# A two-block model: one distance table, ten kept half tiles of weights, and a ring of seven gathers

## Chip, cores and metric

One core of one Trainium2 chip. The metric is the device time of one launch in microseconds, as the median of several runs. One launch computes everything below.

## The reference, cut to what matters

Two blocks of two layers on 256 tokens of width 1024, in float32. The first block (sparse attention, a second attention, two MLPs) is not touched by the change. The second block alternates a mixer and a layer of experts:

```python
for i in range(2):                                  # DEPTH
    shift, scale, gate = ada_mod(c, ada_w[i, 0], ada_b[i, 0])
    h = x * scale + shift
    f = short_conv_mixer(h, ...) if i == 0 else diff_attention(h, ...)
    x = layer_norm(ALPHA * x + gate * f, ...)
    shift, scale, gate = ada_mod(c, ada_w[i, 1], ada_b[i, 1])
    f = peer_ffn(x * scale + shift, ...)
    x = layer_norm(ALPHA * x + gate * f, ...)

# diff_attention, per head h and part p (8 heads, two softmaxes each)
s = einsum('qd,kd->qk', q, k) - slopes[h] * (qpos - kpos)    # slopes[h] = 2**-(h+1)
p = softmax(where(qpos >= kpos, s, -inf)); a = p[0] - lam * p[1]
o = rms_norm(a @ v) ...; return o @ w_o

# peer_ffn: 8 heads choose 16 of 16384 experts each, for every token
act = gelu(einsum('td,thkd->thk', x, u[idx]))
return einsum('thk,thkd->td', g * act, v[idx])
```

Each token thus reads 128 rows of u and of v in either layer; u and v stand side by side in one table of 8 KB rows.

## The kernel before

Every engine has its own program, written out by hand in `build`; semaphores order them. Tokens lie in two tiles of 128.

**Dense part.** Until about 814 us into the span TensorE works through 59 tiles of weights (512 columns each), which SP loads chunk by chunk into `wring` (two tiles deep, loop at L542 to L550). GpSimd meanwhile loads 96 pieces of `ada_w` into a ring of three buffers (L585); the third lies in the memory of `alibi`, and `ada_used` counts the pieces that VectorE has used (L2076). ScalarE loads the distance tables `alibi` once that count is 96 (L1932, L1933). There are eight tables of 128 x 256, one for each head; VectorE adds one to the scores in `masked` (L2639).

**Slots.** The experts' work is 512 slots, in the order layer 0 tile 0, layer 0 tile 1, layer 1 tile 0, layer 1 tile 1, each of 128. For slot s GpSimd gathers one expert's row for each of the 128 tokens, 1024 KB, into buffer s % RING of `g_ring` (`gather`, L596 to L607); VectorE forms the dot products (L2722); ScalarE applies the gelu and the gate and spreads the coefficient on a diagonal (L1740 to L1745); TensorE multiplies the diagonal by the row's other half into a sum in PSUM (`slot`, L1127) and frees the buffer (`slot_used`). GpSimd gathers slot s + RING only then. RING is 8. The first gathers wait for two more things: slot 6 for `hrow_done`, slot 7 for `ln_done`, because the buffer of slot 7 lies where the layer norm before it still works (L610 to L614).

**Parts beside the slots.** The second mixer and the second experts' query projection are cut into 58 parts for each token tile, and `parts_due` gives the slot at which each part has its turn: tile 0 beside slots 128 to 255, tile 1 beside slots 256 to 383. TensorE runs parts three slots ahead (PE_AHEAD). Among the parts are 24 half tiles of weights, 1024 KB each (`half_tile`, L1157 to L1168): 0 to 11 for q, k and v, then attention, then 12 to 15 for the output projection, then 16 to 23 for the queries of the experts. In this trace halves 0 to 11 of tile 0 run at 1190 to 1266 us and of tile 1 at 1565 to 1640; 12 to 15 from 1337 and from 1713; 16 to 23 from 1395 and from 1770.

**Loads of half tiles.** `late_turns` plans them: 48 halves are needed (24 twice), the last four stay in place between the two passes, and so SP issues 44 loads of 1024 KB (`late_load`, L537 to L540). Loads 0 and 1 go to the two buffers `late`, ahead of the query tiles; 2 to 5 to the four halves of `wring`, when the dense part leaves them; every further load waits until the half before it in its buffer has been used. Load 23 goes to the buffer of scores and waits for `idx_ready` (L561). SP issues in order: a load that waits holds all later ones. Counting from the plan, loads 2 to 5 are issued before the first half is used, 6 to 26 during the first pass and 27 to 43 during the second.

**Keys and values.** In the mixer a row of q, k or v is copied from PSUM (`copy_row`, L1785), turned by TensorE (`turn_row`) and copied again (`copy_turned`, L1787 to L1789): q to `dq`, k to `dk`; v goes to `dv` directly. `dk` and `dv` lie in the memory of `whi`.

Of the kernel before, what the change touches and what calls it, by code (L numbers as in the profile page):

```python
# [22 lines left out]
ALU = mybir.AluOpType  # L23
# [21 lines left out]
LAM_INIT = 0.8 - 0.6 * math.exp(-0.3)  # L45
A_HEADS = 8
PEER_HEADS = 8
PEER_KEYS = 128
PK = 16
N_EXPERTS = PEER_KEYS * PEER_KEYS  # L50
SLOTS = PEER_HEADS * PK
RING = 8

# [51 lines left out]
LATE_HALVES = 2 * BESIDE  # L105
FRESH = 2
KEPT = 4
LATE_LOADS = 2 * LATE_HALVES - KEPT
LATE_BUFFERS = 4 + FRESH


def late_turns():


    free = [(b, None) for b in range(LATE_BUFFERS)]
    turns, loads = {}, [0] * (LATE_BUFFERS + 1)
    for j in range(LATE_LOADS):
        if j == LATE_HALVES - 1:
            b, before = LATE_BUFFERS, None
        else:  # L120
            b, before = free.pop(0)
        loads[b] += 1
        turns[j] = (b, loads[b], before)
        if not LATE_HALVES - KEPT <= j < LATE_HALVES:
            free.append((b, j))
    for j in range(LATE_LOADS, 2 * LATE_HALVES):
        turns[j] = turns[j - LATE_HALVES]
    return turns
# [40 lines left out]

def build(nc, xT_in, w_stream, wf_in, c_in, ada_w, tab_in, vec_in, alibi_in, subkeys, experts, lam_in, subln_in, out, out_rows):  # L170
    ctx = ExitStack()
    with ctx:
# [14 lines left out]
        xT = sb("xT", [P, KC, T])  # L187
        at_f = -(-nc.sbuf_base // 32) * 32
        wf = sb("wf", [P, KC, HEADS])
        wfl = twin("wfl", [P, KC, HEADS], at_f)  # L190
# [6 lines left out]
        whi = sb("whi", [P, CPT, KC, P], F32R)  # L197
        dk = aside("dk", [P, KC, SEQ], at_h)
        dv = aside("dv", [P, 2, D], at_h + 4 * KC * SEQ)
        at = -(-nc.sbuf_base // 32) * 32  # L200
# [10 lines left out]
        vec = sb("vec", [P, N_VEC])  # L211
        alibi = sb("alibi", [P, A_HEADS, SEQ])
        adaM = sb("adaM", [P, 4, 24])
# [102 lines left out]
        g_ring = arena[:, 0:RINGN].rearrange("p (r n) -> p r n", r=RING)  # L316
        peer = carve(RINGN)
        pqT = peer(2, 2, SEQ)
# [38 lines left out]
        xnT = m(KC, SEQ)  # L357
        assert m.at[0] <= RINGN
        m = peer
# [52 lines left out]

        late_landed = [sem(f"late_landed{b}") for b in range(LATE_BUFFERS + 1)]
        w_landed = [[sem(f"w_landed{s}_{c}") for c in range(CPT)] for s in range(2)]
# [17 lines left out]
        relu_done, h1_done = sem("relu_done"), sem("h1_done")  # L432
        wf_c_landed, wf_hi, wf_split, f_done = sem("wf_c_landed"), sem("wf_hi"), sem("wf_split"), sem("f_done")
        z_copied, head_rt, head_ri, head_bc, head_done = (
# [84 lines left out]
        def late_half(j):  # L519

            b = LATE[j][0]
            if b < FRESH:
                return late[:, b]
            if b < LATE_BUFFERS:
# [8 lines left out]
        def _(sp):  # L533
# [3 lines left out]
            def late_load(j):  # L537
                i = j % LATE_HALVES
                tile = w_stream[G_QKV + i // 2].rearrange("c p k n -> (c p k n)").rearrange("(h p m) -> h p m", h=2, p=P)
                sp.dma_start(late_half(j), tile[i % 2]).then_inc(late_landed[LATE[j][0]], 16)  # L540
# [17 lines left out]
            for j in range(FRESH, LATE_LOADS):  # L558
                b, _, before = LATE[j]
                if b == LATE_BUFFERS:  # L560
# [17 lines left out]
        def _(pool):  # L578
# [39 lines left out]
        def _(pe):  # L618
# [405 lines left out]
            for x in range(8):  # L1024
# [134 lines left out]
            def half_tile(g, half, dst, lhs):  # L1159

                j = 2 * (g - G_QKV) + half
                b, turn, _ = LATE[j]
                pe.wait_ge(late_landed[b], 16 * turn)
                w = late_half(j)
# [15 lines left out]
            def mixer_parts(t):  # L1180
# [18 lines left out]
                def scores(h):  # L1199
                    for p in range(2):  # L1200
# [5 lines left out]
                        at = h % 2 * SEQ  # L1206
                        mm(banks[4 + p][:, at:at + w], dq[g, h], dk[g, h, 0:w], start=True, stop=True).then_inc(d_s, 1)

# [10 lines left out]
                def values(h):  # L1219
                    n = A_HEADS * t + h  # L1220
                    pe.wait_ge(d_ptc, n + 1)
                    for kt in range(t + 1):
                        last = mm(banks[2 * t + h // 4][:, (h % 4) * P:(h % 4 + 1) * P], d_at[n % 2][:, kt * P:(kt + 1) * P],
                                  dv[:, kt, h * P:(h + 1) * P], start=kt == 0, stop=kt == t)
                    last.then_inc(d_pvd, 1)
# [177 lines left out]
        def _(act):  # L1403
# [192 lines left out]
            act.wait_ge(wf_c_landed, 32)  # L1596
            nc.scalar.copy(wfh[:, :, :], wf[:, :, :]).then_inc(wf_hi, 1)
            af(c_row, c_row, ACT.Silu).then_inc(silu_done, 1)
# [160 lines left out]
            def copy_f(t, q):  # L1759
                n = q // 2 if q < 4 else q - 2  # L1760
                act.wait_ge(slot_used[RING - 1], (n + 1) * (SLOTS // RING))
                for b in range(2):
                    copy_rows(b, q)
# [23 lines left out]
            def copy_turned(k, x, dst):  # L1787
                act.wait_ge(row_turned, k + 1)
                nc.scalar.copy(dst, banks[4 + x % 2][:, :].rearrange("p (c n) -> p c n", c=CPT)).then_inc(turn_copied, 1)  # L1789

            def mixer_parts(t):
                g0 = G_QKV + BESIDE * t
# [4 lines left out]
                for x in range(6):  # L1797
                    if 1 <= x <= 4:
                        y = x - 1
                        copy_turned(8 * t + y, y, dq[:, 4 * y:4 * y + 4] if y < 2 else dk[:, 4 * (y - 2):4 * (y - 2) + 4, tile])  # L1800
# [5 lines left out]
                    copy_row(g0 + x, x, qrow[x % 2] if x < 4 else dv[:, t, (x - 4) * TILE_N:(x - 3) * TILE_N])  # L1806
                    yield
# [201 lines left out]
        def _(dve):  # L2009
# [373 lines left out]
            ada_add(0)  # L2383
            lo_part(wfl[:, :, :], wf[:, :, :], wfh[:, :, :], wf_hi, 1, wf_split)

# [239 lines left out]
            def mixer_parts(t):  # L2625
# [64 lines left out]
            def last_rows():  # L2690
# [3 lines left out]
                for b, half in enumerate(halves):  # L2694
                    if b:
                        dve.wait_ge(slot_used[RING - 1], N_SLOTS // RING)
                    else:
# [169 lines left out]
def _constants():  # L2867
# [22 lines left out]
    dist = (part[:, None] + P - np.arange(SEQ)[None, :]).astype(np.float32)  # L2890
    slopes = 2.0 ** (-(8.0 / A_HEADS) * np.arange(1, A_HEADS + 1, dtype=np.float32))
    alibi = np.stack([np.where(dist >= 0, -s * dist * np.float32(HD ** 0.5), NEG) for s in slopes], 1).astype(np.float32)
    return tab, alibi

# [91 lines left out]
```

## Time and profile before

| | |
|---|---|
| median of 3 runs | 2231.76 us (2231.5 to 2236.64) |
| profiled execution, its own time | 2229.24 us |
| its span | 2227.4 us |
| busy in the span | PE 91%, DVE 71%, ACT 50%, POOL 28% |
| moved by DMA | 762.48 MB, 587.24 MB of it by the queue of GpSimd |

The profile is of one execution. PE is TensorE, PEld its weight load, DVE VectorE, ACT ScalarE, POOL GpSimd, SP SyncE; L605 is line 605 of the kernel. The span is a little shorter than the execution's own time, which includes what lies around it. GB/s is what the 16 DMA engines moved in a stretch. "DMA to landing" is the time from the issue of a transfer to its arrival.

### The profile page before, as it was taken

To read this page: it belongs to the slowest core of one execution; us is meant where nothing else is said; L and a number is where in the kernel's file an instruction comes from. 1 tells how busy PE (TensorE), PEld (TensorE's weight loads), DVE (VectorE), ACT (ScalarE), POOL (GpSimd) and SP (SyncE) were. 2 spreads that over 40 slices of the span, in tenths; PEclk is the share of its full clock that TensorE was granted. 3 is DMA by queue.
4 is the path that set the end of the run, shared out by engine and by line. 5 is a ranking of instruction groups with operands and counts; after the bars stand their busy time and mean duration, and the time that the engine had idled before them with its cause. 6 is when DMAs were issued, how large, how long until landed. Compare 5 with 4: busy or idle time off the path is not lost.

```text
span 2227.4 us, 28567 instructions
## 1 busy us (share of the span) xinstructions
PE 2019.8 (91%) x9930; PEld 1296.7 (58%) x9930; DVE 1583.6 (71%) x3680; ACT 1114.0 (50%) x2714; POOL 630.6 (28%) x621
## 2 busy tenths in 40 slices
PE   8899999999999999888779988998998999788876
PEld 7789999789999975433224434443444443233322
DVE  7867778768788888666676486567568666776655
ACT  5455436466534465454444474454456544444543
POOL 0000011100011044434333343344234444444442
PEclk9899999999999999999999999999999999999999
DMA  6236698726698679999999999999999999999997
GB/s 238 77 96 207 221 341 285 260 80 215 190 359 310 220 274 419 421 421 421 421 422 420 421 418 416 394 421 421 421 421 410 421 390 422 421 421 419 422 420 295
DMA packets 130485, 762.48 MB, mean 342 GB/s; under 512 B 14384, under 2 KB 16176, under 8 KB 59056
## 3 DMA queue, kind: packets, MB, share of 16 engines
q0 software_dynamic: 87552, 587.24, 64.7%
q1 hardware_dynamic: 42080, 172.06, 21.7%
q8 instruction: 72, 1.18, 0.2%
q10 hardware_dynamic: 720, 1.51, 0.2%
q14 instruction: 61, 0.50, 0.1%
HBM read 759.70 MB, written 1.05 MB: 342 GB/s over the span
## 4 chain that ended last, share of the span: by engine, by line
PE 52%; DMA 30%; DVE 10%; ACT 4%; issue 2%; POOL 1%; DVEq 0%; POOLq 0%; ACTq 0%
DMA arena<-experts,arena 28%; PE bank L1127 16%; PE bank L634 8%; PE bank L636 8%; PE bank L635 8%; PE bank L1166 7%; DVE arena L2722 3%; DMA arena<-ada_w 1%; DVE wlo L2029 1%; POOL arena L605 1%; ACT arena L1745 1%; PE bank L818 1%; ACT arena L1531 1%; ACT arena L1744 1%; DVE arena L2164 0%
## 5 line engine op out<-in xcount | busy, mean ns | idle before, releaser
L1127 PE MATMUL bank<-arena 128*128 128x512 f32 x2048 | 979.8, 618 | 149.7 <-ACT arena L1745 149.2
L2722 DVE CUSTOM_DVE_ANT_0 arena<-arena 128x1024 f32<-128x1024 f32 x512 | 626.1, 1224 | 441.9 <-DMA arena<-experts,arena 441.0
L605 POOL DMA_INDIRECT arena<-experts,arena x512 | 566.6, 1107 | 830.8 <-PE bank L1127 778.5
L1127 PEld LDWEIGHTS bank<-arena 128*128 128x128 f32 x2048 | 376.2, 194 | 704.8 <-issue 368.0
L1740 ACT ACTIVATE arena<-arena 128x1 f32<-128x1 f32 x512 | 103.4, 202 | 567.5 <-DVE arena L2722 565.7
L1418 ACT CAST whi<-wring 128x1024 fp32r<-128x1024 f32 x229 | 239.0, 1049 | 225.7 <-PE bank L636 219.4
L2029 DVE TENSOR_TENSOR wlo<-wring,whi 128x1024 fp32r<-128x1024 f32 x229 | 278.7, 1222 | 72.0 <-ACT whi L1418 71.4
L1745 ACT ACTIVATE arena<-tab,arena 128x128 f32<-128x128 f32 x512 | 205.6, 401 | 16.7
L585 POOL DMA_DIRECT2D arena<-ada_w x64 | 34.3, 535 | 567.5 <-DVE adaM L2076 554.8
L634 PE MATMUL bank<-hTh,whi 128*128 128x256 f32 (+1 forms) x584 | 169.9, 291 | 2.5 <-DVE wlo L2029 1.3
L636 PE MATMUL bank<-hTh,wlo 128*128 128x256 f32 (+1 forms) x584 | 165.3, 283 | 0.0
L1744 ACT ACTIVATE arena<-arena 128x1 f32<-128x1 f32 x512 | 150.9, 295 | 16.6
L635 PE MATMUL bank<-hTl,whi 128*128 128x256 f32 (+1 forms) x552 | 155.9, 282 | 0.0
L634 PE MATMUL bank<-mTh,whi 128*128 128x272 f32 (+1 forms) x512 | 146.2, 286 | 2.4 <-DVE mTl L2096 2.4
L635 PE MATMUL bank<-h1l,whi 128*128 128x272 f32 (+1 forms) x512 | 145.8, 285 | 0.0
L635 PE MATMUL bank<-mTl,whi 128*128 128x272 f32 (+1 forms) x512 | 145.8, 285 | 0.0
L634 PE MATMUL bank<-h1h,whi 128*128 128x272 f32 (+1 forms) x512 | 145.6, 284 | 0.0
L636 PE MATMUL bank<-h1h,wlo 128*128 128x272 f32 (+1 forms) x512 | 145.4, 284 | 0.0
L636 PE MATMUL bank<-mTh,wlo 128*128 128x272 f32 (+1 forms) x512 | 145.4, 284 | 0.0
L634 PEld LDWEIGHTS bank<-hTh,whi 128*128 128x128 f32 x584 | 110.1, 189 | 8.9 <-issue 5.3
L636 PEld LDWEIGHTS bank<-hTh,wlo 128*128 128x128 f32 x584 | 110.3, 189 | 0.0
L635 PEld LDWEIGHTS bank<-hTl,whi 128*128 128x128 f32 x552 | 104.0, 188 | 1.0 <-issue 1.0
(412 smaller groups left out, 2940.7 us busy)
## 6 DMA issues: line engine op xcount, KB each, us to landing
wring<-w_stream SPq DMA_DIRECT2D x233, 512.0 KB, 4.2
arena<-ada_w POOLq DMA_DIRECT2D x64, 512.0 KB, 5.6
wring<-w_stream SPq DMA_DIRECT2D x22, 1024.0 KB, 8.9
late<-w_stream SPq DMA_DIRECT2D x21, 1024.0 KB, 8.9
alibi<-ada_w POOLq DMA_DIRECT2D x32, 512.0 KB, 5.5
arena<-experts,arena POOLq DMA_INDIRECT x512, 14.7
xT<-xT_in SPq DMA_DIRECT2D x2, 544.0 KB, 4.3
alibi<-alibi_in ACTq DMA_DIRECT2D x1, 1024.0 KB, 5.0
```

The source lines that it names most:

```text
L605: pool.indirect_dma_start(g_ring[:, r], None, experts[n // (2 * PEER_HEADS)], bass.IndirectOffsetOnAxis(idx[:, s // SLOTS % 2, s % SLOTS:s ...
L634: mm(dst, a[0], b[0], start=start, stop=False)
L635: mm(dst, a[0], b[1], start=False, stop=False)
L636: return mm(dst, a[1], b[0], start=False, stop=stop)
L1127: last = mm(banks[2 * t + b][:, :], diag[:, r], g_ring[:, r, D + b * TILE_N:D + (b + 1) * TILE_N], start=s % SLOTS == 0, stop=s % SLOTS == ...
L1166: last = mm(dst, lhs[:, 4 * half + k], w[:, k * TILE_N:(k + 1) * TILE_N], start=half == 0 and k == 0, stop=half == 1 and k == 3)
L1418: nc.scalar.copy(whi[:, c], wring[:, g % 2, c]).then_inc(hi_done, 1)
L1740: link(af(gel8[:, r:r + 1], act8[:, r:r + 1], ACT.Gelu))
L1744: link(af(coef8[:, r:r + 1], gel8[:, r:r + 1], ACT.Copy, scale=gate[:, s // SLOTS % 2, at:at + 1]))
L1745: af(diag[:, r], ident, ACT.Copy, scale=coef8[:, r:r + 1]).then_inc(diag_ready, 1)
L2029: v.tensor_tensor(wlo[:, g % 2, c], wring[:, g % 2, c], whi[:, c].bitcast(F32), ALU.subtract).then_inc(lo_done, 1)
L2722: v.tensor_tensor_reduce(g_ring[:, r, 0:D], g_ring[:, r, 0:D], hrow[:, t], 1.0, 0.0, ALU.mult, ALU.add, act8[:, r:r + 1]).then_inc(dot_don ...
```

## The change

One table `dist` (128 x 256, the distances alone) takes the place of the eight of `alibi`; the scale of the score operation is multiplied by the head's slope, and q is divided by it when it is copied to `dq`: four activations with a scale in place of one copy. Keys and values of a tile lie together in `dkv`, so that the second tile's half is free until its keys come. `dist` shares its memory with `wf` and waits for `f_done`.

The memory that this frees holds a third buffer `late`, and RING falls to 7; the eighth buffer's place becomes `spare`, a buffer for half tiles, as does the second half of `dkv` for half 5. Ten halves stay in place between the passes (KEPT), so that 38 loads are issued in place of 44. By the new plan loads 0 to 2 go ahead of the query tiles (SP first waits for `ada_used` 96, since the third `late` buffer is the third of the ada ring); 3 goes to `spare` when the layer norm is over; 4 to 8 follow as the dense part ends, 5 (and so 6 to 8 behind it) at its very end; 9 to 23 in the first pass, through three buffers in turn; 28 and 31 to 43 in the second, through five.

```diff
-RING = 8
+RING = 7
-FRESH = 2
-KEPT = 4
-LATE_LOADS = 2 * LATE_HALVES - KEPT
-LATE_BUFFERS = 4 + FRESH
+FRESH = 3
+LATE_SPARE, LATE_SCORES, LATE_KEYS = FRESH + 4, FRESH + 5, FRESH + 6
+KEPT = (0, 1, 2, 3, 5, 6, 20, 21, 22, 23)
+LATE_LOADS = [j for j in range(2 * LATE_HALVES) if j < LATE_HALVES or j - LATE_HALVES not in KEPT]
...
+    free = [(b, None) for b in [*range(FRESH), LATE_SPARE, *range(FRESH, LATE_SPARE)]]
+    for j in range(2 * LATE_HALVES):
+        i = j % LATE_HALVES
+        if j in LATE_LOADS:
+            if i == KEPT[-1]:
+                b, before = LATE_SCORES, None
+            elif j == KEPT[4]:
+                b, before = LATE_KEYS, None
+            else:
+                b, before = free.pop(0)
...
+        if b < LATE_SCORES and (j != i or i not in KEPT):
+            free.append((b, j))
...
-        ada_ring = [first(D), first(D), alibi[:, 0:4].rearrange("p a q -> p (a q)")]
+        ada_ring = [first(D), first(D), late[:, FRESH - 1, 0:D]]
...
                 if g == G_PQ:
+                    sp.wait_ge(ada_used, 96)
                     for j in range(FRESH):
                         late_load(j)
...
+                if b == LATE_SPARE and before is None:
+                    sp.wait_ge(ln_done, KC)
+                elif b == LATE_SCORES:
                     sp.wait_ge(idx_ready, 2 * PEER_HEADS + 1)
+                elif b == LATE_KEYS:
+                    sp.wait_ge(lin_done, CPT * G_QKV)
...
                 if s == 6:
                     pool.wait_ge(hrow_done, 4)
-                elif s == 7:
-                    pool.wait_ge(ln_done, 8)
...
+            def copy_queries(k, y):
+                act.wait_ge(row_turned, k + 1)
+                for c in range(CPT):
+                    h = CPT * y + c
+                    last = af(dq[:, h], banks[4 + y][:, c * P:(c + 1) * P], ACT.Copy, scale=1.0 / SLOPES[h])
+                last.then_inc(turn_copied, 1)
...
-            act.wait_ge(ada_used, 96)
-            act.dma_start(alibi[:, :, :], alibi_in).then_inc(tables_landed, 16)
+            act.wait_ge(f_done, 1)
+            act.dma_start(dist[:, :], dist_in).then_inc(tables_landed, 16)
...
-                        v.tensor_tensor_reduce(d_sm[:, k % 4, 0:w], banks[4 + p][:, h % 2 * SEQ:h % 2 * SEQ + w], alibi[:, h, SEQ - w:SEQ],
-                                               HD ** -0.5, -3.0e38, ALU.add, ALU.max, d_mx[:, k:k + 1]).then_inc(d_smd, 1)
+                        v.tensor_tensor_reduce(d_sm[:, k % 4, 0:w], banks[4 + p][:, h % 2 * SEQ:h % 2 * SEQ + w], dist[:, SEQ - w:SEQ],
+                                               SLOPES[h] * HD ** -0.5, -3.0e38, ALU.add, ALU.max, d_mx[:, k:k + 1]).then_inc(d_smd, 1)
```

Two semaphores of the dense part (`wf_hi`, `wf_split`) become one, and the waits for "the last slot of a tile" are written for a ring that does not divide 128; neither adds a wait.

## Rows read from the trace of the kernel before

**Rows 1.** The page, chain that ended last: shares of the span by line.

```profile
DMA arena<-experts,arena 28%; PE bank L1127 16%; PE bank L634 8%; PE bank L636 8%; PE bank L635 8%; PE bank L1166 7%; DVE arena L2722 3%; DMA arena<-ada_w 1%; DVE wlo L2029 1%; POOL arena L605 1%; ACT arena L1745 1%; PE bank L818 1%; ACT arena L1531 1%; ACT arena L1744 1%; DVE arena L2164 0%
```

**Rows 2.** Line 605, all gathers: count, ns, first and last.

```profile
L605 POOL DMA_INDIRECT arena<-experts,arena x512: 932/937/1989, 806.4 to 2199.9; - x171
```

**Rows 3.** Windows: length, PE, PEld, DVE, ACT, POOL busy, PEclk, DMA share, GB/s.

```profile
814.00:1190.00 376.00, 313.20 (x903) 142.49 (x901) 271.62 (x702) 183.42 (x517) 152.68 (x144) 0.97 1.01 421
1190.00:1268.00 78.00, 77.57 (x194) 35.00 (x194) 37.13 (x99) 30.57 (x85) 21.64 (x19) 1.00 1.01 421
1268.00:1395.00 127.00, 110.01 (x325) 51.10 (x326) 96.40 (x283) 78.17 (x214) 49.49 (x45) 0.97 1.01 417
1395.00:1430.00 35.00, 35.00 (x92) 16.20 (x91) 22.62 (x61) 17.77 (x50) 13.26 (x12) 1.00 0.97 376
1430.00:1571.00 141.00, 124.05 (x323) 55.12 (x322) 95.52 (x246) 67.33 (x190) 59.39 (x53) 0.96 1.01 422
1571.00:1640.00 69.00, 69.00 (x174) 31.25 (x174) 30.95 (x80) 23.21 (x68) 18.71 (x18) 1.00 1.01 421
1640.00:1690.00 50.00, 46.04 (x153) 22.23 (x152) 42.86 (x146) 39.33 (x102) 20.50 (x18) 0.97 1.00 407
1690.00:1770.00 80.00, 70.14 (x208) 33.39 (x207) 57.35 (x136) 43.70 (x115) 33.49 (x28) 1.00 1.01 422
1770.00:1875.00 105.00, 104.63 (x280) 48.74 (x279) 70.58 (x187) 52.44 (x149) 49.45 (x42) 1.00 1.00 405
1875.00:2213.00 338.00, 274.98 (x633) 107.99 (x632) 218.49 (x511) 152.77 (x452) 141.91 (x130) 0.97 1.00 416
```

**Rows 4.** Line 605, the gathers, 1040 to 1130 us: issue to landing.

```profile
DMA to landing us min/median/max: 12.4/15.3/16.3
```

**Rows 5.** Line 605, 1405 to 1420 us: issue to landing.

```profile
DMA to landing us min/median/max: 8.3/10.4/11.8
```

**Rows 6.** The page, DMA issues: KB each, median us to landing.

```profile
late<-w_stream SPq DMA_DIRECT2D x21, 1024.0 KB, 8.9
alibi<-alibi_in ACTq DMA_DIRECT2D x1, 1024.0 KB, 5.0
```

**Rows 7.** Timeline of SP: loads 2 and 5, of four before the first pass.

```profile
851.86 0.33 SPq L540 DMA_DIRECT2D wring<-w_stream  x1
...
951.34 0.33 SPq L540 DMA_DIRECT2D wring<-w_stream  x1
```

**Rows 8.** Line 605, 1240 to 1268 us: count, instruction ns, first and last; landing.

```profile
L605 POOL DMA_INDIRECT arena<-experts,arena x7: 936/938/1691, 1242.4 to 1263.1; - x7
...
DMA to landing us min/median/max: 15.1/16.9/18.9
```

**Rows 9.** Timeline of SP: loads 20 to 22, then 23, then 25 and 26.

```profile
1354.28 44.34 SPq L540 DMA_DIRECT2D wring<-w_stream  x3
...
1423.60 0.33 SPq L540 DMA_DIRECT2D arena<-w_stream  x1
...
1424.44 2.97 SPq L540 DMA_DIRECT2D late<-w_stream  x2
```

**Rows 10.** Tile alibi: its use by VectorE as ada buffer, and its load.

```profile
L2076 DVE CUSTOM_DVE_ANT_0 alibi<-alibi,arena x32: 1149/1218/1227, 178.4 to 717.9; 128x1024 f32<-128x1024 f32 x32
...
L1933 ACTq DMA_DIRECT2D alibi<-alibi_in x1: 444/444/444, 794.8 to 794.8; - x1
```

**Rows 11.** Timeline of ACT: four activations of 128x128, one copy of 128x512.

```profile
1189.72 1.63 ACT L1779 ACTIVATE xT<-xnt,vec 128x128 f32<-128x128 f32 x4
...
1203.24 0.56 ACT L1789 COPY oT<-bank 128x512 f32<-128x512 f32 x1
```

**Rows 12.** Line 540, all loads of half tiles: issue to landing.

```profile
DMA to landing us min/median/max: 7.1/8.9/21.9
```

**Rows 13.** Timeline of PE: halves 7 and 10 of the first pass.

```profile
1236.49 3.60 PE L1166 MATMUL bank<-late,hfT 128*128 128x512 f32 x8
...
1255.81 3.60 PE L1166 MATMUL bank<-wring,hfT 128*128 128x512 f32 x8
```

More of the change, by code:

```diff
@@ L46 @@
 A_HEADS = 8
+SLOPES = [2.0 ** (-(8.0 / A_HEADS) * (h + 1)) for h in range(A_HEADS)]
 PEER_HEADS = 8
@@ L105 @@
 LATE_HALVES = 2 * BESIDE
-FRESH = 2
-KEPT = 4
-LATE_LOADS = 2 * LATE_HALVES - KEPT
-LATE_BUFFERS = 4 + FRESH
+FRESH = 3
+LATE_SPARE, LATE_SCORES, LATE_KEYS = FRESH + 4, FRESH + 5, FRESH + 6
+KEPT = (0, 1, 2, 3, 5, 6, 20, 21, 22, 23)
+LATE_LOADS = [j for j in range(2 * LATE_HALVES) if j < LATE_HALVES or j - LATE_HALVES not in KEPT]
 def late_turns():
[L115 to L119, printed above, removed]
-        else:
[L121 to L124, printed above, removed]
+    free = [(b, None) for b in [*range(FRESH), LATE_SPARE, *range(FRESH, LATE_SPARE)]]
+    turns, loads = {}, [0] * (LATE_SCORES + 1)
+    for j in range(2 * LATE_HALVES):
[7 more added lines that the diff above has]
+                b, before = free.pop(0)
+            at = min(b, LATE_SCORES)
+            loads[at] += 1
+            turns[j] = (b, loads[at], before)
+        else:
+            turns[j] = turns[i]
+        b = turns[j][0]
+        if b < LATE_SCORES and (j != i or i not in KEPT):
             free.append((b, j))
-    for j in range(LATE_LOADS, 2 * LATE_HALVES):
-        turns[j] = turns[j - LATE_HALVES]
     return turns
@@ L167, with build @@
 N_TAB = _tab_layout()
-def build(nc, xT_in, w_stream, wf_in, c_in, ada_w, tab_in, vec_in, alibi_in, subkeys, experts, lam_in, subln_in, out, out_rows):
+def build(nc, xT_in, w_stream, wf_in, c_in, ada_w, tab_in, vec_in, dist_in, subkeys, experts, lam_in, subln_in, out, out_rows):
     ctx = ExitStack()
@@ L211, in build @@
         vec = sb("vec", [P, N_VEC])
-        alibi = sb("alibi", [P, A_HEADS, SEQ])
         adaM = sb("adaM", [P, 4, 24])
@@ L316, in build @@
         g_ring = arena[:, 0:RINGN].rearrange("p (r n) -> p r n", r=RING)
-        peer = carve(RINGN)
+        spare = arena[:, RINGN:RINGN + 2 * D]
+        peer = carve(RINGN + 2 * D)
         pqT = peer(2, 2, SEQ)
@@ L357, in build @@
         xnT = m(KC, SEQ)
-        assert m.at[0] <= RINGN
+        assert m.at[0] <= RINGN + 2 * D
         m = peer
@@ L411, in build @@
         sk_landed = sem("sk_landed")
-        late_landed = [sem(f"late_landed{b}") for b in range(LATE_BUFFERS + 1)]
+        late_landed = [sem(f"late_landed{b}") for b in range(LATE_SCORES + 1)]
         w_landed = [[sem(f"w_landed{s}_{c}") for c in range(CPT)] for s in range(2)]
@@ L432, in build @@
         relu_done, h1_done = sem("relu_done"), sem("h1_done")
-        wf_c_landed, wf_hi, wf_split, f_done = sem("wf_c_landed"), sem("wf_hi"), sem("wf_split"), sem("f_done")
+        wf_c_landed, wf_hi_split, f_done = sem("wf_c_landed"), sem("wf_hi_split"), sem("f_done")
         z_copied, head_rt, head_ri, head_bc, head_done = (
@@ L523, in late_half @@
                 return late[:, b]
-            if b < LATE_BUFFERS:
+            if b == LATE_SPARE:
+                return spare
+            if b == LATE_KEYS:
+                return dkv[:, 1].rearrange("p a n -> p (a n)")
+            if b < LATE_SPARE:
                 ring, half = (1 - (b - FRESH) // 2), (b - FRESH) % 2
@@ L539, in late_load @@
                 tile = w_stream[G_QKV + i // 2].rearrange("c p k n -> (c p k n)").rearrange("(h p m) -> h p m", h=2, p=P)
-                sp.dma_start(late_half(j), tile[i % 2]).then_inc(late_landed[LATE[j][0]], 16)
+                sp.dma_start(late_half(j), tile[i % 2]).then_inc(late_landed[min(LATE[j][0], LATE_SCORES)], 16)
             for g in range(G_QKV):
                 if g == G_PQ:
+                    sp.wait_ge(ada_used, 96)
                     for j in range(FRESH):
@@ L555, in _ @@
                     sp.dma_start(c_row, c_in).then_inc(wf_c_landed, 16)
-            for j in range(FRESH, LATE_LOADS):
+            for j in LATE_LOADS[FRESH:]:
                 b, _, before = LATE[j]
-                if b == LATE_BUFFERS:
+                if b == LATE_SPARE and before is None:
+                    sp.wait_ge(ln_done, KC)
+                elif b == LATE_SCORES:
                     sp.wait_ge(idx_ready, 2 * PEER_HEADS + 1)
+                elif b == LATE_KEYS:
+                    sp.wait_ge(lin_done, CPT * G_QKV)
                 elif before is None:
@@ L1162, in half_tile @@
                 b, turn, _ = LATE[j]
-                pe.wait_ge(late_landed[b], 16 * turn)
+                pe.wait_ge(late_landed[min(b, LATE_SCORES)], 16 * turn)
                 w = late_half(j)
@@ L1206, in scores @@
                         at = h % 2 * SEQ
-                        mm(banks[4 + p][:, at:at + w], dq[g, h], dk[g, h, 0:w], start=True, stop=True).then_inc(d_s, 1)
+                        keys = dkv[g, 0:t + 1, 0, h * P:(h + 1) * P]
+                        mm(banks[4 + p][:, at:at + w], dq[g, h], keys, start=True, stop=True).then_inc(d_s, 1)
                 def turn(h):
@@ L1223, in values @@
                         last = mm(banks[2 * t + h // 4][:, (h % 4) * P:(h % 4 + 1) * P], d_at[n % 2][:, kt * P:(kt + 1) * P],
-                                  dv[:, kt, h * P:(h + 1) * P], start=kt == 0, stop=kt == t)
+                                  dkv[:, kt, 1, h * P:(h + 1) * P], start=kt == 0, stop=kt == t)
                     last.then_inc(d_pvd, 1)
@@ L1596, in _ @@
             act.wait_ge(wf_c_landed, 32)
-            nc.scalar.copy(wfh[:, :, :], wf[:, :, :]).then_inc(wf_hi, 1)
+            nc.scalar.copy(wfh[:, :, :], wf[:, :, :]).then_inc(wf_hi_split, 1)
             af(c_row, c_row, ACT.Silu).then_inc(silu_done, 1)
@@ L1760, in copy_f @@
                 n = q // 2 if q < 4 else q - 2
-                act.wait_ge(slot_used[RING - 1], (n + 1) * (SLOTS // RING))
+                last = (n + 1) * SLOTS - 1
+                act.wait_ge(slot_used[last % RING], last // RING + 1)
                 for b in range(2):
@@ L1799, in mixer_parts @@
                         y = x - 1
-                        copy_turned(8 * t + y, y, dq[:, 4 * y:4 * y + 4] if y < 2 else dk[:, 4 * (y - 2):4 * (y - 2) + 4, tile])
+                        if y < 2:
+                            copy_queries(8 * t + y, y)
+                        else:
+                            keys = dkv[:, t, 0].rearrange("p (h n) -> p h n", h=KC)
+                            copy_turned(8 * t + y, y, keys[:, 4 * (y - 2):4 * (y - 2) + 4])
                     yield
@@ L1805, in mixer_parts @@
                         act.wait_ge(ft_done, 2 * (2 * t) + 2)
-                    copy_row(g0 + x, x, qrow[x % 2] if x < 4 else dv[:, t, (x - 4) * TILE_N:(x - 3) * TILE_N])
+                    copy_row(g0 + x, x, qrow[x % 2] if x < 4 else dkv[:, t, 1, (x - 4) * TILE_N:(x - 3) * TILE_N])
                     yield
@@ L2890, in _constants @@
     dist = (part[:, None] + P - np.arange(SEQ)[None, :]).astype(np.float32)
-    slopes = 2.0 ** (-(8.0 / A_HEADS) * np.arange(1, A_HEADS + 1, dtype=np.float32))
-    alibi = np.stack([np.where(dist >= 0, -s * dist * np.float32(HD ** 0.5), NEG) for s in slopes], 1).astype(np.float32)
-    return tab, alibi
+    near = np.where(dist >= 0, -dist * np.float32(HD ** 0.5), NEG).astype(np.float32)
+    return tab, near
 def kernel(**inputs):
@@ L2954 @@
     vec[:, VEC["eps"][0]:VEC["eps"][0] + 5] = [EPS, HD * EPS, LN_EPS, EPS * EPS, HD * EPS * EPS]
-    tab, alibi = _constants()
+    tab, dist = _constants()
     tokens = np.concatenate([i["meta_tokens"], i["x"][0]], axis=0)
@@ L2965 @@
         "vec_in": vec,
-        "alibi_in": alibi,
+        "dist_in": dist,
         "subkeys": i["peer_sub_keys_2"].transpose(0, 3, 1, 2),
```

12 lines of the change are left out of this document (6 added, 6 removed).

## The prediction, made before the changed kernel was run

> **What bounds the kernel now.** I read the chain of waits first. Its largest share is gathers of experts' rows, followed by the slots that use them (L1127); the half tiles (L1166) come behind the dense part [rows 1]. The gathers begin at 806 us [rows 2], so the change lives in the last 1400 us. Next come the windows, cut where the kind of work changes. The reader should see two things in each row: the GB/s, which stand at 421 nearly everywhere, and PE's busy time against the length. Where PE has idle time at 421 GB/s, the transfers set the pace. Where PE is busy from end to end (1190 to 1268, 1395 to 1430, 1571 to 1640, 1770 to 1875) PE sets it, and the transfers are either level with it (421) or have gaps (376, 405) [rows 3].
>
> Then the landing times of the gathers. With the engines saturated and nothing else running a gather lands 15.3 us after its issue [rows 4], nearly all of it a queue; where the engines have gaps it is 8.3 at the least and 10.4 in the middle [rows 5]. So a ring that runs ahead shows as a shorter landing, and 8.3 us is the floor I use.
>
> **The unit.** A half tile is 1024 KB [rows 6]; at 421 GB/s [rows 3] that is 1.0486 MB / 421 = 2.49 us of all engines. A gather has the same size. Taking every load away at this price would be the sum if transfers bounded everything. They don't, so I go by stretches and keep one number: how much later (+) or earlier (-) the changed kernel is at the stretch's end.
>
> **(a) 814 to 1190, +5.0.** Before, four loads (2 to 5) are issued here, the first at 851.86 and the last at 951.34 [rows 7]; by the new plan it is six (3 to 8). The engines run at 421 GB/s and PE has 63 us idle [rows 3], so two loads more are 2 x 2.49 later. Bounds: 2.5, if load 3 falls into the hole that the later issue of slot 7 leaves, to 7.5, if a ring of seven is once empty beside the dense tiles. SP holds loads 6 to 8 behind load 5 until the dense part ends, but no half is used before 1190.
>
> **(b) 1190 to 1268, 0, and 3.7 carried on.** Twelve halves are used; before, each use starts a load, now only six do (six halves stay): 14.9 us less to move. But PE is busy 77.57 of 78 [rows 3], so the stretch does not shorten. What counts is how far the gathers run ahead. Before, seven are issued in 1242.4 to 1263.1, one in 3.45 us, and land in 16.9 [rows 8]: 16.9 / 3.45 = 4.9 in flight, 3.1 of eight landed. Afterwards, at the floor of 8.3 [rows 5], 2.4 are in flight and 4.6 of seven have landed: 1.5 gathers ahead, 1.5 x 2.49 = 3.7. The other 11 us become gaps, because the ring is full. In 1268 to 1395 PE has 17 us idle at 417 GB/s [rows 3] and as many loads as before, so the 3.7 is taken there. Bounds: 0 to 14.9.
>
> **(c) 1395 to 1430, -3.7.** PE is busy throughout and the engines move 376 GB/s [rows 3]: a gap of 35 x (1 - 376/421) = 3.7 us. The cause stands in SP's timeline: after load 22, at about 1398, SP waits with load 23 until 1423.60 and then issues four loads at once [rows 9]. In the new plan loads 19 to 22 follow the uses of halves 16 to 19, before that wait, and only 23 stands behind it. The loads fill the gap; PE takes the gain in 1430 to 1571, where it has 17 us idle [rows 3]. Bounds: 0 to 7.5 (three loads).
>
> **(d) 1571 to 1640, -2.5, taken after it.** Eleven loads for twelve. PE is busy 69 of 69, so again it is a lead, taken in 1640 to 1690, where PE has 4 us idle [rows 3]. Bounds 0 to 2.5.
>
> **(e) 1640 to 1690, +2.5.** The engines have a gap (407 GB/s [rows 3]): the ring is full. A full ring of seven holds one gather less than one of eight, and what follows is bound by transfers. Bounds 0 to 2.5.
>
> **(f) 1690 to 1770, -2.5.** Three loads for four, at 422 GB/s with 9.9 us of PE idle [rows 3]. Bounds 0 to 2.5.
>
> **(g) 1770 to the end, +2.5.** PE is busy 104.63 of 105 and the engines drop to 405 GB/s [rows 3]. One load fewer in a gap saves nothing. The ring is full again, one gather less lies ahead, and the 338 us behind it are bound by transfers without any load, so that gather is paid. Bounds 0 to 5 (a ring emptied twice).
>
> **At nothing.** The table: `alibi` is loaded at 794.8 [rows 10], lands in 5.0 [rows 6], before the first gather at 806 [rows 2]; its 2.2 us of transfer are hidden by the dense part, and would be gained at most. SP's new wait for 96 ada pieces: the last piece starts on VectorE at 717.9 [rows 10], the query tiles' loads queued behind it come later. The third early load lies in the dense part, two tiles ahead of need. ScalarE's wait for `f_done` is over hundreds of us before. Four activations for one copy: 1.63 against 0.56 us [rows 11], four times 1.07 on ScalarE, which is idle over half of 1190 to 1268 [rows 3]; TensorE's next turn is two halves away. If that cover were gone it would be 4.3 us. Score operations keep their shapes. Slot 7 no longer waits for the layer norm but for slot 0.
>
> **Sum.** 5.0 - 3.7 - 3.7 - 2.5 + 2.5 - 2.5 + 2.5 = -2.4 us. Against the profiled execution (span 2227.4, own time 2229.24) that is 2226.8. The median of the runs is 2.5 higher, and I give the time on its scale: 2231.76 - 2.4 = 2229.4. A measurement of this kernel can tell about 0.3%, 6.7 us, from no change.
>
> **Rival 1: the bytes decide.** Seven loads fewer after 814 (42 to 35) come off in full: 7 x 2.49 = 17.4 us, 2214.4. For it: 416 GB/s or more in 1209 of the 1399 us [rows 3]. Against it: PE's four full stretches, in which six of the loads fall [rows 3]. Halfway cases, where the ring carries more out of (b) than I allow, lie between 2214 and 2225.
>
> **Rival 2, slower: the ring of seven.** If seven buffers leave the gathers no lead (landing stays at 13 us or more in 1240 to 1420), (b), (c), (d) and (f) give nothing and (a), (e), (g) stay: +10.0, 2241.8. It decides as soon as (b) and (c) together bring less than 3 us. For it: at 15.3 us of landing and 2.49 a gather, six of eight are already in flight [rows 4]. Against it: 8.3 us suffices when the queue is short [rows 5].
>
> **Rival 3: weights come late.** The first pass now turns through three buffers: load 10 starts when half 7 has been used, and half 10 must wait for it. Half 7 ends at 1240.1 and half 10 starts at 1255.8 [rows 13]: 15.7 us, against a landing of 8.9 in the middle and 21.9 at worst [rows 12]. At the worst twice it is 2 x 6.2 = 12.4 us more, 2241.8. Against it: the old second pass also turns through three buffers, and no half tile waits for its load in the waits.
>
> **Rival 4: a lone gather is quicker than any row shows.** If it landed in half of 8.3, 1.2 would be in flight at the end of (b), 5.8 landed, 2.7 ahead: 6.7 us in place of 3.7, and 2226.4. The Trainium skill ("DMA: Bandwidth & Descriptors", anatomy of one DMA on the gpsimd path) has a fixed 2.0 us plus the bytes at 436 GB/s, an estimate of 4.4 us for a gather, which is this case. The trace speaks against it: no gather lands under 8.3, with the engines in gaps.
>
> **Numbers.** Forecast 0.42, rival 1 with its halfway cases 0.26, rival 2 0.15, rival 3 0.07, rival 4 0.10. Faster by over 0.3% (below 2225.1): rival 1 and the lower edges of forecast and rival 4, 0.33. Slower (above 2238.5): most of rivals 2 and 3 and a little of the forecast, 0.19. Between: 0.48. The range goes from 2216 (half of rival 1) to 2240; the forecast's own is 2224 to 2236.
>
> **What would show it.** Right: slots start about 5 us later at 1190; 1190 to 1268 keeps its 78 us, with PE full and the GB/s down to about 350; landing near 8 to 10 us there; no gap of transfers at 1395 to 1430; a larger gap at 1770 to 1875 than 405 shows; 338 us from there to the end. Wrong: a shorter 1190 to 1268 (then PE was not its limit), landing at 13 us there (rival 2), a half tile that waits for its load (rival 3), or 421 GB/s held through to the end (rival 1).

## The result and the profile after

| | before | changed |
|---|---|---|
| median of 15 runs each | 2233.85 us (2230.5 to 2237.86) | 2237.19 us (2230.99 to 2242.41) |
| profiled execution, its own time | 2229.24 us | 2236.86 us |
| its span | 2227.4 us | 2235.1 us |
| moved by DMA | 762.48 MB | 755.27 MB |

The ratio is 1.0021, with a 95% interval of 1.0012 to 1.0029: the changed kernel is slower, by 0.0021 x 2233.85 = 4.7 us (the two medians differ by 3.3). The prediction said 2.4 us faster; the time lies in its range, the sign is wrong. 7.2 MB less is moved, so the change does what it says. Executions of one kernel differ by several us: the trace of before is of one of 2229.24 us, below all 15, that of the changed kernel of one near its median. So the two traces differ by 7.6 us, some 3 more than the kernels do. (One execution of the ring of seven alone, 3170.61 us at a granted clock of 0.58, is left out of its median below.)

Where did the time go? The page first. Of the changed kernel, the shares of the chain that ended last:

```profile
DMA arena<-experts,arena 24%; PE bank L1141 16%; PE bank L648 9%; PE bank L650 9%; PE bank L649 9%; PE bank L1180 7%; DVE arena L2750 3%; DMA arena<-ada_w 1%; DVE wlo L2057 1%; ACT arena L1760 1%; ACT L1755 1%; ACT L1765 1%; ACT arena L1759 1%; PE bank L832 1%; ACT arena L1546 1%
```

Against [rows 1] the gathers have lost four points, and nothing new carries weight: the slots are now L1141, the half tiles L1180, and ScalarE's rows are at 1%. So it is the same kind of chain, and the question is where it falls behind. The marks are groups of half tiles (halves 0, 12 and 16 of the first pass, the same of the second) and the last slot. The chain of before, in time (start, length, line):

```profile
1190.43 3.70 PE bank L1166 x8
...
1336.81 3.70 PE bank L1166 x8
...
1394.82 3.43 PE bank L1166 x8
...
1565.68 5.30 PE bank L1166 x8
...
1713.36 3.70 PE bank L1166 x8
...
1770.47 3.43 PE bank L1166 x8
...
2217.19 2.00 PE bank L1127 x4
```

and of the changed kernel:

```profile
1199.32 3.70 PE bank L1180 x8
...
1342.59 3.70 PE bank L1180 x8
...
1401.39 3.43 PE bank L1180 x8
...
1571.75 3.70 PE bank L1180 x8
...
1718.30 3.70 PE bank L1180 x8
...
1776.48 3.43 PE bank L1180 x8
...
2224.80 2.00 PE bank L1141 x4
```

Later by 8.9, 5.8, 6.6, 6.1, 4.9, 6.0 and 7.6 us. By this pair of traces the whole loss, and more, is there at the first half tile; the first pass gives back 2.8 of it, and afterwards the lag stays between 4.9 and 7.6. (1.4 of the 8.9 is there at the first gather, 807.8 against 806.4.)

The windows of the changed kernel, cut at the same work as [rows 3] and with its columns; behind the dots two more, from the dense part:

```profile
816.00:1199.00 383.00, 315.11 (x898) 141.94 (x896) 271.29 (x700) 183.11 (x517) 157.48 (x143) 0.97 1.01 416
1199.00:1277.00 78.00, 77.68 (x194) 35.15 (x196) 37.75 (x102) 30.70 (x91) 18.79 (x19) 1.00 0.89 346
1277.00:1400.00 123.00, 106.65 (x322) 50.31 (x321) 95.60 (x279) 77.48 (x214) 51.54 (x45) 0.99 1.01 421
1400.00:1436.00 36.00, 36.00 (x93) 16.50 (x92) 21.35 (x59) 16.19 (x45) 13.23 (x12) 1.00 1.00 413
1436.00:1577.00 141.00, 124.94 (x327) 57.11 (x326) 97.13 (x248) 69.22 (x196) 54.50 (x53) 0.96 1.01 416
1577.00:1647.00 70.00, 70.00 (x177) 31.80 (x175) 32.20 (x84) 25.45 (x76) 21.65 (x19) 1.00 1.01 411
1647.00:1695.00 48.00, 42.28 (x149) 20.78 (x148) 41.63 (x142) 38.15 (x100) 19.97 (x18) 1.00 1.00 400
1695.00:1776.00 81.00, 71.29 (x207) 34.24 (x206) 58.89 (x142) 44.87 (x118) 31.00 (x28) 0.98 1.01 416
1776.00:1881.00 105.00, 103.41 (x278) 48.33 (x276) 67.61 (x179) 50.24 (x144) 48.63 (x41) 1.00 0.97 386
1881.00:2221.00 340.00, 275.82 (x637) 108.21 (x636) 219.89 (x514) 153.03 (x453) 141.34 (x132) 0.97 1.01 417
...
855.00:860.00 5.00, 5.00 (x29) 3.57 (x28) 5.00 (x14) 3.29 (x10) 0.44 (x1) 1.00 0.67 238
820.00:960.00 140.00, 124.06 (x450) 67.42 (x450) 106.65 (x282) 72.46 (x202) 57.78 (x49) 0.96 1.00 408
```

Read the last column as an account. Engines that move less than 421 GB/s lose the stretch's length times (1 - GB/s / 421). Over the ten stretches of [rows 3] that makes 14.6 us of gaps before; in the ten above, 37.8. So the gaps grew by 23.2 us, while seven loads fewer saved 7 x 2.49 = 17.4: 5.8 us on balance, and the sum of the ten lengths has gone from 1399 to 1405. Every byte saved came back as a gap, and some more. The largest gaps are where PE is busy from end to end: 13.9 us in 1199 to 1277, 8.7 in 1776 to 1881. The last two rows show a new one, of 4.3 us beside the last dense tiles, half of it in 855 to 860. (Dense tiles do not end at 814 us: the last matmul of line 634 starts at 950.8, of line 648 of the changed kernel at 953.2, between the first slots.) The same window of before has no gap:

```profile
820.00:960.00 140.00, 123.56 (x443) 65.90 (x441) 105.92 (x280) 73.44 (x202) 57.59 (x51) 0.98 1.01 421
```

How full the ring is, by the gathers of the changed kernel (line 621) from 1240 to 1275 us:

```profile
L621 POOL DMA_INDIRECT arena<-experts,arena x9: 936/936/1036, 1244.4 to 1272.3; - x9
...
  PE bank L1141: 25.4, 9
...
DMA to landing us min/median/max: 5.2/8.1/11.1
```

and from 1040 to 1130, where the engines are saturated:

```profile
DMA to landing us min/median/max: 10.0/12.8/13.8
```

In the first, every one of the nine gathers waited for TensorE to free its buffer (the row under it), one in 27.9 / 8 = 3.49 us; 8.1 / 3.49 = 2.3 in flight and 4.7 of seven landed. In the second the landing is 2.5 us shorter than in [rows 4]: one gather less in the queue.

SP's timeline of the changed kernel shows loads 3, 4, 5 and 6 to 8, all ahead of the first half tile:

```profile
824.69 0.33 SPq L551 DMA_DIRECT2D arena<-w_stream  x1
...
857.60 0.33 SPq L551 DMA_DIRECT2D wring<-w_stream  x1
...
953.77 0.33 SPq L551 DMA_DIRECT2D dkv<-w_stream  x1
954.15 1.38 SPq L551 DMA_DIRECT2D wring<-w_stream  x3
```

Six where [rows 7] has four, four of them within 2 us.

### The profile page after: what moved, and what is told of

It reads as the page before. It is cut to its first block, busy times and chain, and to the rows that moved or that the text cites. A ratio compares the mean times of both kernels' runs of the same rounds, so it can differ in the third digit from the quotient of the medians.

```text
span 2235.1 us, 28573 instructions
## 1 busy us (share of the span) xinstructions
PE 2019.8 (90%) x9930; PEld 1299.4 (58%) x9930; DVE 1583.8 (71%) x3680; ACT 1114.3 (50%) x2726; POOL 628.8 (28%) x621
## 2 busy tenths in 40 slices
DMA packets 129621, 755.27 MB, mean 338 GB/s; under 512 B 14288, under 2 KB 16208, under 8 KB 59088
## 4 chain that ended last, share of the span: by engine, by line
PE 53%; DMA 26%; DVE 11%; ACT 6%; issue 3%; POOL 1%; SPq 0%; DVEq 0%; POOLq 0%; ACTq 0%
DMA arena<-experts,arena 24%; PE bank L1141 16%; PE bank L648 9%; PE bank L650 9%; PE bank L649 9%; PE bank L1180 7%; DVE arena L2750 3%; DMA arena<-ada_w 1%; DVE wlo L2057 1%; ACT arena L1760 1%; ACT L1755 1%; ACT L1765 1%; ACT arena L1759 1%; PE bank L832 1%; ACT arena L1546 1%
## 5 line engine op out<-in xcount | busy, mean ns | idle before, releaser
L1141 PE MATMUL bank<-arena 128*128 128x512 f32 x2048 | 977.4, 617 | 158.5 <-ACT arena L1760 158.3
L1141 PEld LDWEIGHTS bank<-arena 128*128 128x128 f32 x2048 | 375.3, 194 | 711.8 <-issue 363.5
```

Source lines behind the costliest of these rows:

```text
L1141: last = mm(banks[2 * t + b][:, :], diag[:, r], g_ring[:, r, D + b * TILE_N:D + (b + 1) * TILE_N], start=s % SLOTS == 0, stop=s % SLOTS == ...
```

## The experiments

Three parts may have cost the time: the smaller ring, the table with its extra activations, or loads that come earlier or more thickly than before. The runs take them apart one by one. Each ratio is against the kernel before, on the same chip and in the same set of runs (whose median was 2230.75 us for the first four and 2230.01 for the rest).

**The table alone.** One table, keys and values together, the new wait for the ada pieces; ring of eight and the old plan of 44 loads. Against the changed kernel:

```diff
-RING = 7
+RING = 8
-FRESH = 3
+FRESH = 2
-KEPT = (0, 1, 2, 3, 5, 6, 20, 21, 22, 23)
+KEPT = (20, 21, 22, 23)
...
+                elif s == 7:
+                    pool.wait_ge(ln_done, 8)
```

> One distance table, scaled queries and keys and values side by side as in the change; ring of eight, 44 loads in the old plan. Theory A (the time follows the transfers: bytes moved plus gaps in them): nothing on the way of the transfers changes, so the time is that of before within 0.1% (ratio 0.999 to 1.001). Rival B (the new copies cost TensorE time: four activations for one copy, keys read in two pieces): at least 3 us slower than before, ratio 1.0015 or more, and the first pass (halves 0 to 11) longer than 78 us.

Measured: 2230.1 us, ratio 1.0000 (0.9991 to 1.0009). Its windows:

```profile
820.00:960.00 140.00, 124.07 (x445) 66.08 (x444) 106.03 (x281) 73.56 (x202) 57.15 (x51) 0.98 1.01 421
...
1395.00:1430.00 35.00, 35.00 (x91) 16.20 (x90) 22.62 (x61) 16.50 (x47) 14.35 (x11) 0.99 0.96 362
```

No gap in the dense part, and the old gap at 1395 to 1430 is there as in [rows 3]. The table, the four activations and the new waits cost nothing that the runs can tell: that part of the prediction holds, and the suspicion against them falls. (The interval leaves room for 2 us either way.)

**The ring of seven alone.** The kernel above with one buffer less; its place stays unused.

```diff
-RING = 8
+RING = 7
...
-                elif s == 7:
-                    pool.wait_ge(ln_done, 8)
```

> As table_alone, but a ring of seven; the plan of 44 loads is the old one. Theory A: a gap of 1 to 3 us beside the dense tiles at 850 to 900 us and larger gaps where TensorE is busy without loads (1395 to 1430, 1640 to 1690, 1770 to 1875), together 5 to 8 us: ratio to before 1.002 to 1.0035. Rival C (seven buffers are enough, the ring costs nothing, and all of the loss is the order of the loads): ratio 0.999 to 1.001.

Measured: 2237.82 us, ratio 1.0032 (1.0020 to 1.0043), 7.1 us slower by the ratio. No load is added or moved. Its windows:

```profile
820.00:960.00 140.00, 121.35 (x454) 67.19 (x453) 103.78 (x274) 69.58 (x195) 53.24 (x46) 0.96 0.99 406
...
855.00:860.00 5.00, 5.00 (x32) 3.91 (x31) 5.00 (x10) 3.32 (x8) 0.00 (x0) 1.00 0.55 175
```

The gap beside the dense tiles is there without any change of loads: for 5 us PE is busy throughout and GpSimd issues nothing (0.00). Its timeline shows why (start, length, instruction; in brackets how long it had waited and for whom):

```profile
851.24 1.10 POOL L621 DMA_INDIRECT arena<-experts,arena  x1 [6.16 <-PE bank L1141]
860.12 1.41 POOL L621 DMA_INDIRECT arena<-experts,arena  x1 [7.78 <-PE bank L1141]
```

Two gathers in succession wait 6 and 8 us for TensorE to free a buffer. In the first wait TensorE itself waits for a coefficient (3.23 us, until 846.86); in the second it works on a dense tile (849.65 to 857.96). With eight buffers there is one such wait (7.56 us before the gather at 854.00), and the engines don't run dry. So the gap is not made by the extra early loads.

By the runs the ring alone explains a loss as large as the change's. That it is paid in this gap is shown only in part. This trace is of an execution of 2244.68 us, above its median; its first half tile starts at 1197.59, against 1190.47 in the table alone, but 2.8 of these 7.1 us are there at the first gather (809.5 against 806.7). The runs with load 23 last (further down) have the same code as these two up to half 16, and so give a second trace of each. With seven buffers the first half tile then starts at 1193.72, with eight at 1192.72, and the windows are, seven first:

```profile
820.00:960.00 140.00, 121.97 (x448) 66.47 (x447) 104.96 (x279) 71.05 (x198) 55.76 (x48) 0.98 1.01 413
...
820.00:960.00 140.00, 123.49 (x447) 67.27 (x446) 106.07 (x282) 72.22 (x202) 55.36 (x50) 0.96 1.00 415
```

Gaps of 2.7 and 2.0 us: eight buffers can have one too. Right ahead of it the granted clock is below 1.00. First the row of that run (eight buffers, load 23 last), then of the ring of seven alone:

```profile
845.00:850.00 5.00, 5.00 (x20) 3.60 (x21) 4.98 (x16) 3.88 (x8) 0.94 (x1) 0.66 1.01 419
...
845.00:850.00 5.00, 3.14 (x5) 1.51 (x5) 5.00 (x21) 2.78 (x7) 0.08 (x1) 0.58 1.01 426
```

Part of these 5 us thus ran at the 1.2 GHz level, after 5 us in which TensorE was busy for 2.19 and 3.19; the table alone has 1.00 there after 3.71, but before has 1.00 after 2.87. In this row all four traces with seven buffers have 0.53 to 0.73, and of five with eight only this one is below 1.00, so the lower clock may itself come of the ring. No run separates the two.

Nor is the ring's loss in this place alone. Against their partners with eight buffers the two kernels with a ring of seven and the old loads move 414 for 421 and 416 for 419 GB/s from 816 to 1180 us (6.1 and 2.6 us more of gaps), but also 413 for 416 and 415 for 417 from 1180 to 2210 (7.3 and 4.9 us). Of the larger gaps that the expectation named there, at the same work of the ring of seven alone, one shows: 404 for 419 GB/s at 1640 to 1690, but 360 for 362 and 399 for 400 at the other two.

**The ring of eight with the rest of the change.** The changed kernel with eight buffers, hence without `spare`: nine halves stay, 39 loads, and five of them (3 to 7) in place of six ahead of the first pass.

```diff
-RING = 7
+RING = 8
-KEPT = (0, 1, 2, 3, 5, 6, 20, 21, 22, 23)
+KEPT = (0, 1, 2, 5, 6, 20, 21, 22, 23)
-    free = [(b, None) for b in [*range(FRESH), LATE_SPARE, *range(FRESH, LATE_SPARE)]]
+    free = [(b, None) for b in range(LATE_SPARE)]
...
+                elif s == 7:
+                    pool.wait_ge(ln_done, 8)
```

> The change with a ring of eight: no spare buffer, nine halves kept (all but 3), 39 loads, three ahead. Theory A: five loads before the first pass (four before): 2.5 us later there, no gap beside the dense tiles; 1200 to 1280 keeps its 78 us with a gap of 10 to 14 us, and about 4 to 6 us are carried on; in all 3 to 6 us faster than before, ratio 0.997 to 0.999, and 6 to 10 us faster than the change. Rival C (order of the loads alone): about the change's time less half of its loss, ratio 1.000 to 1.002.

Measured: 2226.53 us, ratio 0.9975 (0.9964 to 0.9986): faster than before by 5.6 us and, between the ratios, by 0.0046 x 2231 = 10 us than the changed kernel, though it moves one load more. (One load less stands ahead of the first pass, which may be 2.5 of the 10.) Its windows:

```profile
820.00:960.00 140.00, 124.20 (x452) 67.16 (x451) 107.88 (x288) 75.68 (x209) 59.00 (x52) 0.98 1.01 421
...
1193.00:1271.00 78.00, 77.73 (x189) 35.19 (x190) 37.71 (x101) 28.82 (x90) 19.11 (x19) 0.98 0.90 349
```

No dense gap. The chain has its first half tile at 1193.27, 2.8 us later than before (one load more is 2.5), and half 12 at 1336.07, 0.7 earlier: 3.5 us are carried out of the stretch that moves 349 GB/s. That is near the prediction's terms (a), 2.49 a load, and (b), 3.7, with the ring kept.

**The loads held back.** If transfers cost time where they set the pace and nothing where PE is full, loads 4 to 8 should be issued while the first halves run, not ahead of them. The changed kernel, ring of seven, with a later wait for these five:

```diff
+HELD = {4: 0, 5: 1, 6: 2, 7: 3, 8: 4}
...
+                if j in HELD:
+                    sp.wait_ge(lin_done, CPT * G_QKV + 2 * HELD[j] + 2)
```

> The change as it is, but loads 4 to 8 are held until halves 0 to 4 of the first pass have been used, one after each. Theory A: five loads of 2.49 us leave the stretch that transfers bound and fill the 14 us gap beside halves 0 to 11; no lead is carried out of it any more (3 us): about 9 us faster than the change, 2227 to 2230 us on the scale of before's 2233.85, ratio to before 0.997 to 0.9985; GB/s in 1190 to 1270 back above 410. Rival D (the loads ahead of the first pass are hidden, the ring alone decides): the time of the change, ratio 1.002. Rival E (halves then wait for their loads): slower than the change, with TensorE idle between halves.

Measured: 2229.12 us, ratio 0.9996 (0.9986 to 1.0007). Between the ratios that is 0.0025 x 2231 = 5.6 us better than the changed kernel, in the direction expected, but less than expected. Its windows:

```profile
820.00:960.00 140.00, 124.91 (x458) 68.69 (x457) 106.55 (x283) 73.50 (x203) 57.74 (x49) 0.96 0.97 400
...
1190.00:1268.00 78.00, 77.42 (x192) 34.92 (x192) 38.03 (x103) 31.12 (x91) 22.73 (x19) 1.00 1.00 408
```

The second row is the point: the stretch takes up five loads (346 to 408 GB/s) in the same 78 us. Halves 0 and 12 start at:

```profile
1190.58 3.70 PE bank L1183 x8
...
1334.88 3.70 PE bank L1183 x8
```

That is 144.3 us, for 143.3 in the changed kernel: five loads, 12.4 us of transfer, cost 1.0 there. The first half starts 8.7 us earlier, not 12.4. Of the 3.7 between them 2.7 are in the dense gap, which has grown to 140 x (1 - 400/421) = 7.0 us, and 0.9 are there at the first gather (808.7 against 807.8). The loads may have filled part of what the ring of seven leaves; the granted clock, 0.53 in 845 to 850, is low here too.

**Load 23 last.** Term (c) of the prediction by itself: the table alone, with load 23 issued behind 24 to 26, so that no load waits behind it.

```diff
-            for j in LATE_LOADS[FRESH:]:
+            for j in sorted(LATE_LOADS[FRESH:], key=lambda j: 26.5 if j == 23 else j):
```

> table_alone (ring of eight, old plan) with one thing moved: SP issues load 23, which waits for idx_ready, behind loads 24 to 26 and not ahead of them. It tests term (c) by itself. Theory A1 (as the prediction had it): the gap of 4 to 5 us at 1395 to 1430 closes and is gained: 2 to 4 us faster than before, ratio 0.998 to 0.999. Theory A2 (the ring is then less full when TensorE's busy stretch of 1454 to 1495 begins, and gaps appear there instead): no gain, ratio 0.9995 to 1.0005.

Measured: 2230.28 us, ratio 1.0001 (0.9992 to 1.0011). Its windows:

```profile
1395.00:1430.00 35.00, 35.00 (x94) 16.30 (x93) 21.30 (x59) 16.35 (x46) 13.29 (x11) 1.00 1.01 422
...
1540.00:1545.00 5.00, 5.00 (x13) 2.94 (x13) 4.23 (x11) 3.59 (x10) 0.00 (x0) 0.50 1.01 421
1545.00:1550.00 5.00, 5.00 (x12) 2.18 (x11) 4.93 (x17) 1.24 (x5) 2.76 (x3) 0.92 0.81 295
```

The gap of 1395 to 1430 is gone (362 to 422 GB/s, 4.9 us), but no time comes of it. From half 16 to the next half 0 it is now 170.8 us (1397.02 to 1567.78), without the edit 169.3 (1396.50 to 1565.81) and in the trace of before 170.9. A new gap of 1.5 us stands at 1545 to 1550, where PE is busy 5.00 of 5 and VectorE 4.93, and the window from 1500 to 1565 moves 408 GB/s in place of 421. The reading nearest to these rows is that filling the gap lets the transfers run ahead only until they meet the next stretch that compute fills.

**The same with seven buffers.** `RING = 7` and load 23 last; the edits are those shown above.

> ring_seven_alone with load 23 behind 24 to 26. Theory A1: as with a ring of eight, 2 to 4 us faster than ring_seven_alone (ratio to before about 1.0015 to 1.0025). Theory A2': with seven buffers there is no room for the lead, so the closed gap is given back before 1580: the ratio of ring_seven_alone, 1.003.

Measured: 2239.29 us, ratio 1.0046 (1.0032 to 1.0060); the interval overlaps that of the ring alone. With either ring no gain from moving load 23 shows. Against the same kernel with eight buffers seven cost 0.0045, again 10 us.

**Both findings together.** Ring of eight, nine halves kept, and loads 3 to 7 held until halves 0 to 4 have been used:

```diff
+HELD = {3: 0, 4: 1, 5: 2, 6: 3, 7: 4}
...
+                if j in HELD:
+                    sp.wait_ge(lin_done, CPT * G_QKV + 2 * HELD[j] + 2)
```

> ring_eight (nine kept, three ahead) with loads 3 to 7 held until halves 0 to 4 have been used. Theory A: no load is left in the stretch before the first pass that transfers bound (four before, five in ring_eight): 8 to 12 us earlier than ring_eight at the first half, less a gap of 1 to 4 us beside the dense tiles; the lead of about 3 us out of the first pass is lost: in all 5 to 8 us faster than ring_eight, 2219 to 2222 on the scale of before's 2230.75, ratio 0.9945 to 0.9965. Rival D (an early load costs nothing with eight buffers): the time of ring_eight, 0.9975. Rival E (halves wait for loads): slower than ring_eight.

Measured: 2219.22 us, ratio 0.9951 (0.9937 to 0.9965): 11 us faster than before and, between the ratios, 16 faster than the changed kernel. Its windows:

```profile
820.00:960.00 140.00, 126.92 (x474) 70.10 (x473) 112.29 (x296) 79.08 (x217) 60.94 (x53) 0.99 1.01 418
...
1183.00:1261.00 78.00, 77.96 (x200) 35.40 (x200) 37.06 (x100) 30.95 (x90) 22.75 (x19) 1.00 1.01 421
```

The first half tile starts at 1183.04, 10.2 us earlier than in the ring of eight with the rest of the change, and half 12 at 1329.40, 6.7 earlier: the lead of 3.5 us out of the stretch is given up, since its engines are now saturated, but the loads no longer stand in a stretch where transfers set the pace. The halves kept in place and the loads held beat both kernels; the change as made paid for its halves with a ring buffer.

## Why the prediction was wrong

**How far the steps can be read.** They come from one trace of each kernel. Traces of the same code differ too: at the first half tile by 2.3 us with eight buffers (1190.47 and 1192.72) and by 3.9 with seven (1197.59 and 1193.72). So the steps below show where to look; that a step failed is shown where runs bear it out, which they do for the ring and for (c).

**What held.** The bound was read rightly, and four signs came as named: 1199 to 1277 kept its 78 us with PE full at 346 GB/s (about 350 forecast), the gathers land in 8.1 us there (8 to 10), the gap of 1395 to 1430 has nearly closed (376 to 413 GB/s), and 1776 to 1881 has a larger one (405 to 386). Two did not: the slots are 8.9 us later at the first half, not about 5, and the end takes 340 us, not 338. (b)'s lead of 3.7 came as 3.1 at half 12 and 2.3 at half 16. No half waits for its load in the waits (rival 3), and the bytes did not decide (rival 1).

**The ring of seven, 5.0 said in all, 7 to 10 measured.** This is the first step that failed. The sum has the ring in (e) and (g), 2.5 each; three pairs of runs, seven buffers against eight, put it at 0.0032, 0.0045 and 0.0046 (7.1, 10 and 10 us, the last with a load moved as well). In (a) the prediction put it at nothing, and "a ring of seven is once empty beside the dense tiles" only into the upper bound. (a) came as 8.9 for 5.0 (7.5 without the 1.4 that lies ahead of it), with a gap of 4.3 where the ring runs empty. Loads here cost about what they move: the ring of eight's one more came to 2.8, 2.0 of it behind the first gather. With 5.0 for the two loads, 2.5 of the 7.5 are left for the ring and the lower clock beside it; the two traces without a load added have 4.3 and 0.5 from the first gather to the first half. The term was worked out over 376 us as a whole; at the scale of a single dense tile TensorE frees no buffer for 6 to 8 us, and there the lead of the ring counts.

**(c), -3.7 said, -0.5 measured, and (f), -2.5 said, +1.1 measured.** (c) is the second step that failed, and with the two went the sign: the gap closes, but its gain does not arrive. "PE takes the gain in 1430 to 1571, where it has 17 us idle" took the idle time of a long window as room at every point of it. In the run with load 23 last the gap closes with nothing else changed, and the ratio is 1.0001. By that trace a later stretch in which TensorE and VectorE are both full stops the transfers instead. (f) counted a load removed from 1690 to 1770 in the same way; its window shows 416 GB/s where 422 stood, but no run tests it.

**(d), (e) and (g)** together came within 2.1 us of their sum: -1.2 for (d) and (e), where 0 was said, and +1.6 for (g), where +2.5 was. By step the sum misses by 3.9 (a), 1.4 (b), 3.2 (c), -1.2 (d, e), 3.6 (f) and -0.9 (g): 10.0 us, from -2.4 to the +7.6 of this pair of traces; by the ratio it misses by 7.1. That (d), (e) and (g) fit is partly luck: the ring's cost, which two of them stand for, was larger and lay in part ahead of them.

**Rival 2** came nearest in size and was weighed too low. Its mark, a landing of 13 us or more in 1240 to 1420, did not come (10.1 in the middle); its point of decision did, by these two traces: (b) and (c) brought 2.8 us, less than its 3. The prediction weighed the ring by the lead in the PE-full stretches, where the gathers land in time with seven buffers, and not by the places where eight were just enough.

**What stays open.** In the run with load 23 last, which engine ends 1396 to 1566 was not settled. Ahead of the new gap TensorE's granted clock is 0.50, its 1.2 GHz level, from 1540 to 1545, after 5 us in which it was busy for 1.83; the kernel without the edit has 0.76 in that row, after 2.18. That may be part of it. What a ring of eight leaves of the dense gap differs too (421 GB/s in 820 to 960 in three profiles, 418 and 415 in two more), and how much of the gap is the clock's, with either ring, stays open. So does where the rest of the ring's cost lies, behind 1180 us. A ring of nine was not tried.

## What to carry to other kernels

Account a stretch by its bytes and its gaps. In this kernel a transfer removed where compute was full only became a gap, and a gap filled there was worth at most the lead that the buffers could hold until transfers set the pace again. Move transfers from stretches that they pace into stretches that compute fills before removing any, and don't pay for it with the buffers that carry the lead. Look at a ring at its narrowest places, a few microseconds at a time, and not only by the mean over a window. Take a second trace of the same code before reading a difference of a few microseconds between two.

## What was not expected of the hardware

A gather of 1024 KB can land much sooner than the 8.3 us that was the shortest in the trace of before: 5.2 us in 1240 to 1275 above. Rival 4 had set 4.4 us beside it, worked out from the Trainium skill ("DMA: Bandwidth & Descriptors", anatomy of one DMA on the gpsimd path); the trace of the changed kernel comes to within 0.8 us of that estimate at its shortest, so the prediction's remark that the trace speaks against it rested on a trace without so short a queue. The median of 8.1 us, which sets the lead, did stay at the floor that the sum used.
